# Forget gates of an attention layer: the 16 weight columns made the stationary operand, the result turned afterwards

## The chip, the cores and the metric

The kernel runs as one program on one core of a Trainium2 chip. The metric is the device time of one execution in microseconds (us); several executions of each kernel are compared by their median.

## What is computed

The program is two blocks of a transformer in float32, for one sequence of 512 tokens with 1024 features. The first block has a dilated window attention beside a retention, an attention over a memory, and a mixture of 32 experts. The second block has two layers: the even one with a differential and a sparse attention, the odd one with the forgetting attention below; each is followed by a layer norm, an MLP of width 4096 and another layer norm. The change lies in the odd layer's forget gates:

```python
h = x @ w_in_odd[li]                       # 512 x 3088: q, k, v of 16 heads of 64, and 16 forget logits
qf, kf, vf, fl = _split(h, ODD_SPLITS)
...
log_f = jax.nn.log_sigmoid(f_logit + f_bias)
c = jnp.cumsum(log_f, axis=1).transpose(0, 2, 1)
s = jnp.einsum('bqhd,bshd->bhqs', qb, kf) + cq[..., None] - c[:, :, None, :]
p = jax.nn.softmax(jnp.where(mask, s, -jnp.inf), axis=-1)
```

## The kernel before

The kernel is written engine by engine: one function per engine and stage, which issue instructions in a fixed order, and semaphores that are counted in a first pass over the program. `T` is TensorE, `A` ScalarE, `V` VectorE, `G` GpSimd, `Y` SyncE, which issues the loads.

**Projections.** A product in float32 is made of three products in the type fp32r: features and weights are each split into a high part and a low part (what the high part leaves), and high x high, low x high and high x low are summed in the same bank (`three`, `products`, L448 to L455). `FH` and `FL` are the features' parts, features on the partitions, in 8 blocks of 128 features with 512 tokens each. Weights come in units of 4 blocks x 512 columns: SyncE loads unit u into one of four buffers `R`, ScalarE copies it to the high part (`act_cut`, L434), VectorE subtracts for the low part (`dve_cut`, L442), in one of two split buffers `W`. SyncE, ScalarE and VectorE wait in `sp_send` and the two cuts for buffers to come free. Two units make one panel of 512 output columns. `projecting` takes the four tiles of 128 tokens through the first unit, then through the second: 4 x 12 matmuls each, with a tile's features stationary (128 columns) and the weights moved (512 columns). Each tile fills one of eight PSUM banks.

**Banks.** `Banks.take` hands out banks in rotation. Each set of banks named by `of` has its own turn: projections take from banks 0 to 5 (PANELS), transposes of finished panels from 6 and 7 (FLIPS), and everything else from all eight (ALL). A bank may be taken again when its last user's reader is done, and TensorE waits for that at the take. In the traces' tile names the banks are `PB`.

**The odd layer's projection** (`pe_odd`, `act_odd`, `dve_odd`) has six panels p: q in 0 and 1, k in 2 and 3, v in 4 and 5. ScalarE copies tiles of panels 0 to 3 out of PSUM (L3041), TensorE turns them during the next panel (`pe_turn`, L467), ScalarE stores them (L645); VectorE copies panels 4 and 5 (L3076).

**The forget gates** come after panel 0. The 16 weight columns `k.o_wf`, 8 blocks of 128x16 in plain float32, are not part of the panels. TensorE takes one bank from ALL and, for each tile of 128 tokens, makes 16 products (8 blocks, high and low features read as plain float32) with the tile's features stationary and the 16 columns moved (`group`, L460). The logits lie in the bank with tokens on partitions. `dve_forget` (L3104 to L3120) adds the bias and, with two steps of ScalarE (L3050, L3052), forms the log of the sigmoid in a widened table `o_lw`. After panel 1, TensorE sums it over the tokens with a triangular table, 4 plain float32 products of 512 columns into a bank of ALL, and `dve_forget_sums` (L3127, L3128) reads that bank. On VectorE these two lines stand behind both weight splits of panel 2. GpSimd then makes a selection table (L3135). The attention takes banks from ALL for scores, transposed weights and sums. The output projection `out_odd` starts inside it; VectorE adds its tiles to `X` (L1284) and does the layer norm; TensorE turns the result into the features of the last MLP, banks 6 and 7, and ScalarE and VectorE split them (L542, L552). The MLP's first products take banks from ALL.

```python
        if p == 0:
            bank = k.banks.take(T, ("flog",), k.dve_step.at("forget", "logits"))
            T.wait_ge(*k.c6_in.at(3))
            for i in range(NT):
                at = slice(128 * i, 128 * i + 128)
                ins = group(te, bank[:, 16 * i:16 * i + 16],
                            [(F[:, c, at].bitcast(F32), k.o_wf[:, c, :]) for F in (k.FH, k.FL) for c in range(KT)])
```

Of the kernel before, what the change touches and what calls it, by code (L numbers as in the profile page):

```python
# [284 lines left out]
class Kernel:  # L285


    def __init__(self, nc, ctx, a, out):
# [12 lines left out]
        def both(name, shape):  # L301
# [16 lines left out]
        self.mem_feats = [nc.alloc_sbuf_tensor_at(name, [P, KT, 256], FR, offset=self.z_at + 4 * at)  # L318
                          for name, at in (("mem_hi", 4096), ("mem_lo", 6144))]
        self.pickr = nc.alloc_sbuf_tensor_at("pickr", [P, 16, P], FR, offset=self.z_at + 4 * 13056)  # L320
        self.om = [sb(f"om{i}", [P, D]) for i in range(2)]
        self.ident = sb("ident", [P, P])
        self.mh = sb("mh", [P, 32])
# [153 lines left out]


def projecting(k, name, p, u0, nt, ready, until, between=None, after=None, by_tile=False, steps=None, early=0,
               feats=None):  # L480

# [6 lines left out]
    for n, (half, i) in enumerate(steps):  # L490
# [12 lines left out]
        if half == 1:  # L503
            ins.then_inc(*done.tick(name, p, i))
            if after:
                after(i)
        elif not [x for x in steps[n + 1:] if x[0] == 0]:
            ins.then_inc(*k.w.half_used.tick(u))
            if between:
                between()  # L510
        if n < early:
            yield
            if n == early - 1:
                for tile in {i for _, i in steps[:early]}:
                    k.banks.release((name, p, tile))
# [2431 lines left out]
def odd_views(k):  # L2947
# [3 lines left out]
    k.o_vf = Z[:, 8192:12288].rearrange("p (i d) -> p i d", i=4)  # L2951
    k.o_wf = Z[:, 12288:12416].rearrange("p (k n) -> p k n", k=8)
    k.o_lf, k.o_fb = Z[:, 12416:12480], Z[:, 12480:12496]
    k.o_lw = Z[:, 15616:16128].rearrange("p (i m) -> p i m", i=4)
    k.o_tri = Z[:, 13056:13952]
    k.o_pick = Z[:, 13056:15104].rearrange("p (h m) -> p h m", h=16)
# [21 lines left out]
def pe_odd(k):  # L2978
    T, te, u0 = k.T, k.T.e, k.start["odd"]

    def turn(p):
        return lambda i: pe_turn(k, ("odd", p, i), k.nsp[i], k.panel_a.at("odd", p, i))

    for p in range(6):
        pe_project(k, "odd", p, u0 + 2 * p, NT, lambda i: featured(k, ("ln", 1), i),
                   lambda i: (k.panel_a if p < 4 else k.panel_v).at("odd", p, i), after=(turn(p - 1) if 1 <= p < 5 else None))
        if p == 0:
            bank = k.banks.take(T, ("flog",), k.dve_step.at("forget", "logits"))
            T.wait_ge(*k.c6_in.at(3))
            for i in range(NT):  # L2990
                at = slice(128 * i, 128 * i + 128)
                ins = group(te, bank[:, 16 * i:16 * i + 16],
                            [(F[:, c, at].bitcast(F32), k.o_wf[:, c, :]) for F in (k.FH, k.FL) for c in range(KT)])
            ins.then_inc(*k.pe_step.tick("forget"))
        if p == 1:
            bank = k.banks.take(T, ("fsum",), k.dve_step.at("sums"))
            T.wait_ge(*k.dve_step.at("forget", "wide"))
            group(te, bank[:], [(k.o_lw[:, c, :], k.o_tri[:, 384 - 128 * c:896 - 128 * c])
                                for c in range(4)]).then_inc(*k.pe_step.tick("sums"))
# [32 lines left out]
def act_odd(k):  # L3032
    A, ae, u0 = k.A, k.A.e, k.start["odd"]
    for p in range(6):
        act_cut(k, u0 + 2 * p + 2)
        for i in range(NT):
            if p < 4:
                A.wait_ge(*k.projected.at("odd", p, i))
# [30 lines left out]
def dve_odd(k):  # L3069
    V, ve, u0 = k.V, k.V.e, k.start["odd"]  # L3070
    for p in range(6):
        dve_cut(k, u0 + 2 * p + 2)
        if p >= 4:
            for i in range(NT):
# [28 lines left out]
def dve_forget(k):  # L3103

    V, ve, tb, lf = k.V, k.V.e, k.tmp[0], k.o_lf
    l3 = lf.rearrange("p (i h) -> p i h", i=4)
    V.wait_ge(*k.c6_in.at(3))
    V.wait_ge(*k.pe_step.at("forget"))
    ve.tensor_tensor(l3, k.banks["flog",][:, 0:64].rearrange("p (i h) -> p i h", i=4),
                     k.o_fb.unsqueeze(1).to_broadcast([P, 4, 16]), ALU.add).then_inc(*k.dve_step.tick("forget", "logits"))  # L3110
    V.wait_ge(*k.dve_step.at("forget", "logits"))
    V.settle(ve.tensor_scalar(tb[:, 0:64], lf, -1.0, None, ALU.mult))
# [198 lines left out]
```

## Time and profile before

| what | value |
|---|---|
| runs | 2473.95, 2473.32, 2466.71 us; median 2473.32 |
| profiled execution | 2466.64 us, of it span from first to last instruction 2465.3 us |
| TensorE matmul busy | 2285.8 us, 93% of the span |
| TensorE weight loads, busy | 1686.8 us, 68% |
| VectorE, ScalarE, GpSimd busy | 1044.6, 703.7 and 95.4 us |
| mean granted TensorE clock | 0.960 of full |

PE is TensorE (PEld its weight loads), DVE VectorE, ACT ScalarE, POOL GpSimd, SP SyncE. Times in the trace are microseconds from the start of the span, durations of single instructions may overlap on TensorE, since matmuls are pipelined and their ends are modelled. Names of a matmul are written result <- moved, stationary; its shape is stationary (rows * columns), then moved. The granted clock is a share of full speed: its two levels are 1.2 and 2.4 GHz.

### The profile page before, as it was taken

To read this page: it belongs to the slowest core of one execution; us is meant where nothing else is said; L and a number is where in the kernel's file an instruction comes from. 1 tells how busy PE (TensorE), PEld (TensorE's weight loads), DVE (VectorE), ACT (ScalarE), POOL (GpSimd) and SP (SyncE) were. 2 spreads that over 40 slices of the span, in tenths; PEclk is the share of its full clock that TensorE was granted. 3 is DMA by queue.
4 is the path that set the end of the run, shared out by engine and by line. 5 is a ranking of instruction groups with operands and counts; after the bars stand their busy time and mean duration, and the time that the engine had idled before them with its cause. 6 is when DMAs were issued, how large, how long until landed. Compare 5 with 4: busy or idle time off the path is not lost.

```text
span 2465.3 us, 28479 instructions
## 1 busy us (share of the span) xinstructions
PE 2285.8 (93%) x11871; PEld 1686.8 (68%) x11871; DVE 1044.6 (42%) x1904; ACT 703.7 (29%) x1188; POOL 95.4 (4%) x96
## 2 busy tenths in 40 slices
PE   8998899979989889899788899999899998999998
PEld 7866687754434333587555688888787776888886
DVE  5347365342323222534576633344511455442334
ACT  4333354311100000223355223132113362331330
POOL 2001001010000000000000000000000000000000
PEclk9989999989999999999888999999989999999999
DMA  5232243259999999522100333322222201323220
GB/s 193 86 135 73 95 154 120 80 220 411 426 428 426 427 428 428 181 70 69 69 1 2 103 104 102 103 86 102 81 70 85 86 2 35 109 97 103 91 97 34
DMA packets 106740, 370.34 MB, mean 150 GB/s; under 512 B 15040, under 2 KB 20672, under 8 KB 94320
## 3 DMA queue, kind: packets, MB, share of 16 engines
q1 hardware_dynamic: 103584, 361.65, 39.0%
q0 software_dynamic: 3024, 6.83, 0.9%
q8 instruction: 96, 1.57, 0.3%
q14 instruction: 36, 0.29, 0.0%
HBM read 368.38 MB, written 4.19 MB: 151 GB/s over the span
## 4 chain that ended last, share of the span: by engine, by line
PE 80%; DMA 9%; DVE 7%; ACT 2%; issue 1%; POOL 0%; SPq 0%; DVEq 0%; ACTq 0%; POOLq 0%
PE PB L450 53%; PE PB L1892 9%; PE PB L467 5%; PE PB L460 4%; PE PB L766 4%; PE PB L658 3%; DMA FL_raw<-in_w_exp_gate 3%; DMA FH_raw<-in_w_exp_gate 3%; DMA Z<-in_w_exp_gate 1%; DMA W_raw<-in_w_exp_down 1%; PE PB L782 1%; DVE W L442 1%; PE PB L663 1%; ACT W L434 1%; ACT nsp L692 1%
## 5 line engine op out<-in xcount | busy, mean ns | idle before, releaser
L442 DVE TENSOR_TENSOR W<-R,W 128x2048 fp32r<-128x2048 f32 (+1 forms) x128 | 291.3, 2277 | 668.2 <-ACT W L434 668.1
L450 PE MATMUL PB<-W,FH 128*128 128x512 f32 (+1 forms) x1792 | 557.4, 393 | 16.7 <-DVE FL L820 6.7
L434 ACT ACTIVATE W<-R 128x2048 fp32r<-128x2048 f32 (+1 forms) x128 | 243.4, 1902 | 670.6 <-PE PB L450 666.5
L450 PEld LDWEIGHTS PB<-W,FH 128*128 128x128 f32 x1792 | 331.6, 190 | 86.4 <-DVE FL L820 8.0
L450 PE MATMUL PB<-W,hid 128*128 128x512 f32 x1536 | 350.3, 389 | 5.1 <-DVE W L442 3.3
L450 PE MATMUL PB<-W,FL 128*128 128x512 f32 (+1 forms) x896 | 348.0, 388 | 0.0
L450 PEld LDWEIGHTS PB<-W,hid 128*128 128x128 f32 x1536 | 287.9, 188 | 66.4 <-DVE W L442 4.2
L450 PE MATMUL PB<-FH,W 128*128 128x512 f32 (+1 forms) x1152 | 326.2, 369 | 1.5 <-DVE FL L552 1.5
L450 PEld LDWEIGHTS PB<-FH,W 128*128 128x128 f32 x1152 | 211.3, 192 | 36.6 <-DVE FL L552 1.8
L450 PE MATMUL PB<-FL,W 128*128 128x512 f32 (+1 forms) x576 | 212.2, 368 | 0.0
L450 PEld LDWEIGHTS PB<-W,FL 128*128 128x128 f32 x896 | 169.5, 189 | 34.9
L1892 PE MATMUL PB<-R,om 128*64 128x512 f32 x320 | 150.4, 626 | 16.4 <-DMA FL_raw<-in_w_exp_gate 9.2
L1892 PE MATMUL PB<-Z,om 128*64 128x512 f32 x304 | 124.4, 610 | 0.8 <-issue 0.8
L450 PEld LDWEIGHTS PB<-FL,W 128*128 128x128 f32 x576 | 110.6, 192 | 17.5
L692 ACT ACTIVATE nsp<-nsp,stat 128x512 f32<-128x512 f32 (+3 forms) x146 | 83.4, 572 | 102.5 <-DVE stat L674 102.4
L467 PEld LDWEIGHTS PB<-ident,nsp 128*128 128x128 f32 x674 | 81.6, 150 | 42.5 <-issue 28.4
L467 PE MATMUL PB<-ident,nsp 128*128 128x128 f32 x674 | 104.4, 284 | 5.1 <-ACT nsp L692 2.8
L658 PE MATMUL PB<-Z 64*128 64x512 f32 (+4 forms) x416 | 97.8, 534 | 10.7 <-DVE Z L807 5.1
L766 PE MATMUL PB<-ptr,Z 128*64 128x128 f32 (+1 forms) x768 | 82.5, 290 | 22.6 <-ACT ptr L716 12.1
L674 DVE CUSTOM_DVE_ANT_0 nsp<-PB,Z 128x512 f32<-128x512 f32 (+3 forms) x146 | 69.1, 511 | 62.1 <-PE PB L658 46.2
L1965 ACT ACTIVATE tmp_r<-PB 128x512 fp32r<-128x512 f32 x32 | 17.4, 594 | 262.7 <-PE PB L1892 262.7
L766 PEld LDWEIGHTS PB<-ptr,Z 128*64 128x64 f32 (+1 forms) x768 | 62.0, 149 | 41.7 <-issue 29.7
(329 smaller groups left out, 2632.9 us busy)
## 6 DMA issues: line engine op xcount, KB each, us to landing
R<-in_mlp_w_up SPq DMA_DIRECT2D x32, 1024.0 KB, 5.3
R<-in_mlp_w_down SPq DMA_DIRECT2D x32, 1024.0 KB, 5.0
Z<-in_w_exp_down SPq DMA_DIRECT2D x14, 2048.0 KB, 29.3
Z<-in_w_exp_up SPq DMA_DIRECT2D x13, 2048.0 KB, 35.2
R<-in_w_exp_gate SPq DMA_DIRECT2D x11, 2048.0 KB, 33.8
W_raw<-in_w_exp_up SPq DMA_DIRECT2D x10, 2048.0 KB, 31.5
R<-in_w_exp_up SPq DMA_DIRECT2D x9, 2048.0 KB, 30.9
R<-in_w_in SPq DMA_DIRECT2D x12, 1024.0 KB, 5.8
```

The source lines that it names most:

```text
L434: k.A.e.activation(w.splits[w.split_of[u]][0][:, 0:m], w.rows(u), ACT.Copy).then_inc(*w.hi.tick(u))
L442: k.V.e.tensor_tensor(wl[:, 0:m], w.rows(u), wh[:, 0:m].bitcast(F32), ALU.subtract).then_inc(*w.lo.tick(u))
L450: ins = te.matmul(bank, l, r, start=(start and n == 0), stop=(stop and n == len(terms) - 1), skip_group_check=True)
L460: ins = te.matmul(bank, l, r, start=(n == 0), stop=(n == len(pairs) - 1))
L467: ins = k.T.e.transpose(bank[0:s.shape[1], 128 * n:128 * n + m], s, k.ident[0:m, 0:m])
L658: ins = k.T.e.matmul(bank[:, 0:t.n], t.q, t.keys, start=True, stop=(t.more is None))
L663: k.T.e.matmul(bank[:, 0:t.n], *t.more, start=False, stop=True).then_inc(*k.scored.tick(*t.key))
L674: V.e.tensor_tensor_reduce(ns[:, 0:t.n], k.banks[("scores",) + t.key][:, 0:t.n], t.tab, 1.0, FAR, ALU.add, ALU.min, peak(k, m)).then_inc(* ...
L692: k.A.e.activation(ns[:, 0:t.n], ns[:, 0:t.n], ACT.Exp, bias=peak(k, m), scale=-1.0, accum_out=t.den).then_inc(*k.exped.tick(*t.key))
L766: ins = T.e.matmul(k.banks["sums", *t.bank[0]][t.rows, at], l, r, start=first, stop=last, skip_group_check=True)
L782: ins = T.e.matmul(bank[rows, 128 * c:128 * c + 128], col, k.ident[:], start=True, stop=True, skip_group_check=True)
L1892: ins = T.e.matmul(bank[64 * side:64 * side + 64, :], lhs[:, 128 * c + 64 * side:128 * c + 64 * side + 64], ws[side][:, c, at], start=(c = ...
```

## The change

The 16 columns of weights are split like the panels' weights, by ScalarE (high part) and VectorE (low part), into two small buffers `forget_w` at a free place of `Z`. After panel 0, TensorE makes 8 x 3 = 24 fp32r products with 16 weight columns stationary and all 512 tokens of a block moved, into 16 partitions of one bank taken from ALL. VectorE copies the 16x512 to `o_gates`. After the first two tiles of panel 1 (`behind`, with n = 1), TensorE takes a second bank of ALL and transposes four pieces of 16x128, so that the logits again have tokens on partitions, 128 columns apart. `dve_forget` reads them from there.

```diff
+        self.forget_w = [nc.alloc_sbuf_tensor_at(name, [P, KT, 16], FR, offset=self.z_at + 4 * at)
+                         for name, at in (("forget_hi", 16128), ("forget_lo", 16256))]
...
 def projecting(k, name, p, u0, nt, ready, until, between=None, after=None, by_tile=False, steps=None, early=0,
-               feats=None):
+               feats=None, behind={}):
...
+        if n in behind:
+            behind[n]()
         if n < early:
...
+    k.o_gates = k.tmp[0][0:16, 512:1024]
...
+    def turn_gates():
+        bank = k.banks.take(T, ("flog",), k.dve_step.at("forget", "logits"))
+        T.wait_ge(*k.dve_step.at("forget", "copied"))
+        flips(k, bank, [k.o_gates[:, 128 * i:128 * i + 128] for i in range(NT)]).then_inc(*k.pe_step.tick("forget"))
+
     for p in range(6):
         pe_project(k, "odd", p, u0 + 2 * p, NT, lambda i: featured(k, ("ln", 1), i),
-                   lambda i: (k.panel_a if p < 4 else k.panel_v).at("odd", p, i), after=(turn(p - 1) if 1 <= p < 5 else None))
+                   lambda i: (k.panel_a if p < 4 else k.panel_v).at("odd", p, i), after=(turn(p - 1) if 1 <= p < 5 else None),
+                   behind=({1: turn_gates} if p == 1 else {}))
         if p == 0:
-            bank = k.banks.take(T, ("flog",), k.dve_step.at("forget", "logits"))
-            T.wait_ge(*k.c6_in.at(3))
-            for i in range(NT):
-                at = slice(128 * i, 128 * i + 128)
-                ins = group(te, bank[:, 16 * i:16 * i + 16],
-                            [(F[:, c, at].bitcast(F32), k.o_wf[:, c, :]) for F in (k.FH, k.FL) for c in range(KT)])
-            ins.then_inc(*k.pe_step.tick("forget"))
+            bank = k.banks.take(T, ("gates",), k.dve_step.at("forget", "copied"))
+            T.wait_ge(*k.dve_step.at("forget", "parts"))
+            terms, (wh, wl) = [], k.forget_w
+            for c in range(KT):
+                terms += three((wh[:, c, :], wl[:, c, :]), (k.FH[:, c, :], k.FL[:, c, :]))
+            products(te, bank[0:16, :], terms, True, True).then_inc(*k.pe_step.tick("gates by head"))
...
+        if p == 0:
+            A.wait_ge(*k.c6_in.at(3))
+            ae.activation(k.forget_w[0][:], k.o_wf, ACT.Copy).then_inc(*k.act_step.tick("forget", "high"))
...
+        if p == 0:
+            V.wait_ge(*k.act_step.at("forget", "high"))
+            ve.tensor_tensor(k.forget_w[1][:], k.o_wf, k.forget_w[0][:].bitcast(F32), ALU.subtract).then_inc(
+                *k.dve_step.tick("forget", "parts"))
         dve_cut(k, u0 + 2 * p + 2)
...
+    V.wait_ge(*k.pe_step.at("gates by head"))
+    ve.tensor_copy(k.o_gates, k.banks["gates",][0:16, :]).then_inc(*k.dve_step.tick("forget", "copied"))
     V.wait_ge(*k.c6_in.at(3))
     V.wait_ge(*k.pe_step.at("forget"))
-    ve.tensor_tensor(l3, k.banks["flog",][:, 0:64].rearrange("p (i h) -> p i h", i=4),
+    ve.tensor_tensor(l3, k.banks["flog",][:].rearrange("p (i m) -> p i m", i=4)[:, :, 0:16],
```

Where the instructions now stand is shown at three places of TensorE's order; rows of the change have line numbers two to five higher. `PB2` is bank 2, `W0` and `W1` are the split buffers, `FH` and `FL` the features' parts, `Z` holds tables and weights.

Behind panel 0, before (the last of panel 0, the gates' products, the first of panel 1):

```order
L450 MATMUL PB5<-W0_51,FL_50 128x512
L460 MATMUL PB2<-Z,FH_49 128x16 [waits c6_in,panel_a]
L460 MATMUL PB2<-Z,FH_49 128x16 x7
L460 MATMUL PB2<-Z,FL_50 128x16 x8
L450 MATMUL PB0<-W1_52,FH_49 128x512 [waits added,w_lo]
```

and with the change, to the transposes within panel 1 (three of the 24 products, then the starts of panel 1's tiles):

```order
L452 MATMUL PB5<-W0_51,FL_50 128x512
L452 MATMUL PB2<-FH_49,forget_hi_59 16x512 [waits dve_step,panel_a]
L452 MATMUL PB2<-FL_50,forget_hi_59 16x512
L452 MATMUL PB2<-FH_49,forget_lo_60 16x512
L452 MATMUL PB0<-W1_52,FH_49 128x512 [waits added,w_lo]
L452 MATMUL PB1<-W1_52,FH_49 128x512 [waits added]
L469 MATMUL PB3<-ident,tmp0 128x16 [waits dve_step,panel_a]
L469 MATMUL PB3<-ident,tmp0 128x16 x3
L452 MATMUL PB2<-W1_52,FH_49 128x512 x2
```

The row with 7 or 8 of the same stands for 128 products in all before; there are 24 now, and four transposes into PB3 further down.

Between panel 1 and panel 2, before (the last transposes, the sums over tokens, panel 2's first products):

```order
L467 MATMUL PB7<-ident,nsp3 128x128 [waits panel_a,piece]
L467 MATMUL PB7<-ident,nsp3 128x128 x3
L460 MATMUL PB3<-Z 128x512 [waits dve_step,panel_a]
L460 MATMUL PB3<-Z 128x512 x3
L450 MATMUL PB4<-W1_52,FH_49 128x512 [waits w_lo]
```

and with the change:

```order
L469 MATMUL PB7<-ident,nsp3 128x128 [waits panel_a,piece]
L469 MATMUL PB7<-ident,nsp3 128x128 x3
L462 MATMUL PB4<-Z 128x512 [waits dve_step]
L462 MATMUL PB4<-Z 128x512 x3
L452 MATMUL PB4<-W1_52,FH_49 128x512 [waits dve_step,w_lo]
```

The sums moved from PB3 to PB4, and panel 2's first tile, which is PB4 in both, has a wait for VectorE more.

At the last MLP, before (the last transposes of the features, in PB6 and PB7, and the first products):

```order
L467 MATMUL PB6<-ident,X 128x128 [waits feat_lo,ln_out]
L467 MATMUL PB6<-ident,X 128x128 x3
L467 MATMUL PB7<-ident,X 128x128 [waits feat_lo]
L467 MATMUL PB7<-ident,X 128x128 x3
L450 MATMUL PB2<-FH_49,W1_52 128x256 [waits res,w_lo]
```

and with the change:

```order
L469 MATMUL PB6<-ident,X 128x128 [waits feat_lo,ln_out]
L469 MATMUL PB6<-ident,X 128x128 x3
L469 MATMUL PB7<-ident,X 128x128 [waits feat_lo]
L469 MATMUL PB7<-ident,X 128x128 x3
L452 MATMUL PB7<-FH_49,W1_52 128x256 [waits res,w_lo,feat_lo]
```

The MLP's first bank moved from PB2 to PB7, the bank of the transposes just ahead, with a wait for the features' low parts.

## Rows read from the trace of the kernel before

**Rows 1.** The page: busy time of the engines, and the chain by engine.
```profile
PE 2285.8 (93%) x11871; PEld 1686.8 (68%) x11871; DVE 1044.6 (42%) x1904; ACT 703.7 (29%) x1188; POOL 95.4 (4%) x96
PE 80%; DMA 9%; DVE 7%; ACT 2%; issue 1%; POOL 0%; SPq 0%; DVEq 0%; ACTq 0%; POOLq 0%
```

**Rows 2.** Source line L460, 1780 to 1870: duration ns min/median/max, first and last start, shapes.
```profile
L460 PE MATMUL PB<-Z,FH x64: 177/374/374, 1806.2 to 1826.4; 128*128 128x16 f32 x64
L460 PE MATMUL PB<-Z,FL x64: 262/374/374, 1807.9 to 1829.8; 128*128 128x16 f32 x64
L460 PE MATMUL PB<-Z x8: 592/592/697, 1856.3 to 1859.4; 128*128 128x512 f32 x8
```

**Rows 3.** Chain of waits, 1780 to 1960: start us, us, what.
```profile
1806.31 23.87 PE PB L460 x128
1830.19 15.39 PE PB L450 x60
...
1860.04 13.64 PE PB L450 x60
```

**Rows 4.** Windows: PE, PEld (DVE, ACT, POOL) busy, clock, DMA; the first, L1892 alone.
```profile
600.00:650.00 50.00, 40.97 (x190) 13.27 (x186) 1.00 1.01 426
...
1805.90:1830.20 24.30, 24.30 (x131) 24.23 (x130) 2.29 (x1) 2.40 (x2) 0.00 (x0) 0.58 0.14 44
1830.20:1850.00 19.80, 19.80 (x85) 16.22 (x86) 4.14 (x9) 5.50 (x8) 0.00 (x0) 0.91 0.08 20
```

**Rows 5.** Timeline of TensorE: start us, us, what, count [idle before <-releaser].
```profile
1805.47 0.62 PE L450 MATMUL PB<-W,FH 128*128 128x512 f32 x2
...
1806.15 1.85 PE L460 MATMUL PB<-Z,FH 128*128 128x16 f32 x16
...
1830.03 1.20 PE L450 MATMUL PB<-W,FH 128*128 128x512 f32 x2
...
1856.34 3.70 PE L460 MATMUL PB<-Z 128*128 128x512 f32 x8 [0.75 <-ACT nsp L3041]
1859.47 1.03 PE L450 MATMUL PB<-W,FH 128*128 128x512 f32 x2
```

**Rows 6.** Timeline of VectorE, 1780 to 1870.
```profile
1797.48 2.29 DVE L442 TENSOR_TENSOR W<-R,W 128x2048 fp32r<-128x2048 f32 x1 [9.49 <-ACT W L434]
1808.78 2.29 DVE L442 TENSOR_TENSOR W<-R,W 128x2048 fp32r<-128x2048 f32 x1 [9.01 <-ACT W L434]
1830.29 0.23 DVE L3109 TENSOR_TENSOR Z<-PB,Z 128x64 f32<-128x64 f32 x1 [19.22 <-PE PB L460]
...
1858.61 2.29 DVE L442 TENSOR_TENSOR W<-R,W 128x2048 fp32r<-128x2048 f32 x1 [11.41 <-ACT W L434]
1860.82 0.68 DVE L3127 CAST sums<-PB 128x512 fp32r<-128x512 f32 x1
1861.53 0.68 DVE L3128 TENSOR_TENSOR sums<-PB,sums 16x512 fp32r<-16x512 f32 x1
```

**Rows 7.** Timelines of VectorE and TensorE at the first output product.
```profile
2038.97 0.29 DVE L674 CUSTOM_DVE_ANT_0 nsp<-PB,Z 128x128 f32<-128x128 f32 x1
...
2040.27 0.69 PE L450 MATMUL PB<-W,FH 128*128 128x512 f32 x2 [1.45 <-ACT ptr L716]
```

**Rows 8.** Timelines of TensorE and VectorE in the output projection's second half.
```profile
2074.63 0.74 PE L450 MATMUL PB<-W,FH 128*128 128x512 f32 x2 [1.52 <-DVE X L1284]
...
2080.40 0.69 DVE L1284 SCALAR_TENSOR_TENSOR X<-X,PB 128x512 f32<-128x512 f32 x1 [0.33 <-PE PB L450]
...
2085.85 0.69 DVE L1284 SCALAR_TENSOR_TENSOR X<-X,PB 128x512 f32<-128x512 f32 x1 [0.61 <-PE PB L450]
...
2092.19 0.69 DVE L1284 SCALAR_TENSOR_TENSOR X<-X,PB 128x512 f32<-128x512 f32 x1 [0.30 <-PE PB L450]
```

**Rows 9.** Timelines of TensorE and VectorE at the last MLP's start.
```profile
2103.68 0.56 PE L450 MATMUL PB<-FH,W 128*128 128x256 f32 x1
...
2104.69 0.69 DVE L552 TENSOR_TENSOR FL<-PB,FH 128x512 fp32r<-128x512 f32 x1 [0.16 <-ACT FH L542]
```

## The prediction

> **What bounds the kernel now.** I read the page first: TensorE is busy for 93% of the span and holds 80% of the chain that ended last [rows 1]. So time taken out of TensorE's row of instructions is time off the end, unless a wait replaces it. Next I read the source line of the gates' products: 128 matmuls that move 16 columns each, median 0.374 us [rows 2]. The chain of waits shows them standing on the path alone: 23.87 us between panel 0 and panel 1 [rows 3]. The windows show what they do to TensorE's clock: granted 0.58 over that block and 0.91 over the 20 us behind it; a stretch with 64-column weights that moves 512 columns holds 1.00 [rows 4]. The timelines [rows 5 to 9] then give starts for each step below. For one product of the three-term kind I take the pitch of the panels: three of them start every 0.68 us (1805.47 to 1806.15), so 0.227 us each [rows 5].
>
> **1. The block.** Removed: from 1806.15 to 1830.03, 23.88 us [rows 5]. Added in its place: 8 feature blocks x 3 terms = 24 matmuls that move 512 columns over 16-column weights, 24 x 0.227 = 5.44 us. No row shows such a matmul. Its lower end: nothing shortens the 512 columns that stream by, and the 0.227 us already hides a 128-column weight load, so I put 24 x 0.21 = 5.1 us, an estimate from that row. Its upper end is as if it ran like the plain f32 rows: two instructions per product, 0.427 us each at full clock (8 of them in 3.70 us, less the tail), so 24 x 0.85 = 20.5 us [rows 2, 5]. I take 5.44, since type and moved shape are the panels' own. Term: -18.4 us.
> The Trainium skill (TensorE: Matmul & The Clock Gate, Back-to-back issue gap) puts a warm matmul at its columns over 2.4 GHz plus 2.5 ns, which is 0.216 us here; the panels' row says 0.227. By the page the block would take 5.18 us and the sum would be 0.3 us lower.
>
> **2. The slow clock behind it.** Panel 1's first 60 matmuls take 15.39 us; 60 of panel 2's take 13.64 [rows 3]. The difference, 1.75 us, goes with the low clock if the new block streams without a gap. Term: -1.75.
>
> **3. Turning the result.** After two tiles of panel 1, four transposes are added. The nearest is four transposes of 128x128, whose issue adds 0.44 us to the row of panels; I take 0.44, between 0.1 and 0.8. They wait for nothing. VectorE's copy of 16x512 costs what its 16x512 row costs, 0.68 [rows 6], and starts when the products end: by then the split of 1808.78 is done (1811.07). So it is ready near 1812.5 of the old count, and TensorE asks for it after 24 more products, at 1817.0. The logits' bank PB3 is next wanted 12 products later, 2.7 us after the transposes; VectorE's logits take 0.23 us [rows 6]. Also hidden: ScalarE's high part and VectorE's low part of 128x128 weights, some 0.3 us each (the 128x128 row of [rows 7] is 0.29). They stand ahead of VectorE's split that ended at 1799.77 [rows 6] and is now wanted at 1811.6; if that cover were gone they would cost 0.6. Term: +0.44.
>
> **4. The banks.** One more bank is taken from the rotation of eight, so every later taker of that rotation moves by one. This costs what no line of the diff says. The sums' bank was PB3 and is now PB4. Two things follow. The sums no longer wait for ScalarE's copy out of PB3 (0.75 us idle [rows 5]). But PB4 is panel 2's first bank, so panel 2 now waits for VectorE to have read the sums, behind a weight split that VectorE must do first: 1858.61, then 1860.82, then 1861.53 + 0.68 = 1862.21 [rows 6]. None of these three hangs on the sums' matmuls, which would end 0.7 us earlier. With 0.15 us from VectorE's end to TensorE's start, panel 2 starts at 1862.36 where it started at 1859.47; since a start after a pause is a real start and the old one was queued behind slow f32 passes (first pair 1.03 us long against some 0.73), the loss is 2.6 us. Term: +2.6.
>
> **5. The same shift further on.** In the attention the waits keep their kinds, with bank numbers one higher. At the output projection three things differ. (a) Its first bank waited 1.45 us for ScalarE's copy of turned weights, until 2040.27; PB2 is now freed by VectorE's peak, which ends at 2039.26, so TensorE can start at 2039.4: -0.85 [rows 7]. (b) Tile 1 of the second half waited 1.52 us for a bank that VectorE's last addition frees. Now tile 2 meets that bank, when it is long free. VectorE, which sets the end here, gains only its own small waits for TensorE (0.33, 0.61, 0.30 us at three tiles): -1.2 [rows 8]. (c) The last MLP's first bank was PB2 and is now PB7, which holds the transposed features of the last tile. TensorE therefore waits until VectorE has read them, 2104.69 + 0.69 + 0.14 = 2105.52, where it started at 2103.68: +1.85 [rows 9].
>
> **Sum.** -18.4 - 1.75 + 0.44 + 2.6 - 0.85 - 1.2 + 1.85 = -17.3 us. Against the profiled execution's 2466.64 that is 2449.3. The three runs shown have a median of 2473.32, 6.7 above it; I carry the difference over: 2456.0.
>
> **Rivals.**
> *The clock falls all the same* (14%). 16 of 128 columns hold weights, fewer than any row shows, and there is the new pause of term 4. For it: the old block, continuously issued, lost the clock. Against it: that block moved 16 columns at a time, while 64-column weights with 512 moved keep 1.00 [rows 4]. Price: at half clock (1.2 instead of 2.4 GHz) the block takes at most twice its 5.44 us, and term 2 is not earned: -17.3 + 5.4 + 1.75 = -10.1, or 2463.2. If only the pause before panel 2 costs it the clock, one recovery: 2457.8.
> The Trainium skill (Perfetto Trace Analysis, Matmul Optimizations) says that the engine's power follows its utilization; read as the share of the array in use it would give this rival, read as back-to-back issue my forecast.
> *The bank waits don't bite* (8%): VectorE reaches the sums earlier, or TensorE's queue covers the pause. Without terms 4 and 5c the gain is some 21 us, 2451.6, or a little above. Against it: the split before the sums follows ScalarE's, which follows TensorE's last product.
> *The narrow products run like plain f32* (4%), since no row shows this type with fewer than 128 weight columns. At full clock: 20.5 - 5.44 = 15.1 us back, -2.2, about 2471: no change. At half clock: twice 20.5, 41 us, term 2 not earned, -17.3 + 35.6 + 1.75 = +20, or 2493: **slower**. The change turns slower once one product costs over 5.44/24 + 17.3/24 = 0.95 us.
> *Something behind gives back some of it* (4%): weights, sent four units ahead, or VectorE's layer norm, already the chain at the output projection, take some 7 us: 2463.
> My forecast keeps 70%.
>
> **How the numbers follow.** The likeliest is 2456.0. Its own spread is about 2.5 us from the estimates, and the runs shown lie 7 us apart by themselves, which carries the low end to 2447. The clock rival carries the high end to 2463.2. A measurement of this kernel can tell about 0.3%, 7.4 us, from no change. Forecast, missing waits, clock and most of the giving back are all beyond that: faster 0.94. The f32 case at full clock and a larger giving back make 0.03 same, the f32 case at half clock and what I have not seen 0.03 slower.
>
> **What would show it.** In the new profile: 24 matmuls of 128*16 128x512 that start 0.227 us apart at clock 1.00, about 5.4 us from panel 0 to panel 1; panel 1's first 60 matmuls in 13.6; four small transposes without idle time ahead; no TensorE wait for ScalarE before the sums, but one of 2.5 to 3 us for VectorE's line of the sums before panel 2; no wait of 1.5 us for VectorE's addition in the output projection; a wait of 1.8 us for the features' low parts before the last MLP. The forecast is wrong if the narrow products start over 0.3 us apart, if the clock falls in them, or if TensorE has a new wait outside these places.

## The result, and the profile after

| | before | after |
|---|---|---|
| median | 2473.32 us (2466.71 to 2475.32, 5 runs) | 2456.44 us (2454.54 to 2458.8, 5 runs) |
| ratio of the two | | 0.9935, 95% interval 0.9919 to 0.995 |
| profiled execution | 2466.64 us, span 2465.3 | 2456.44 us, span 2454.8 |

The change is faster by 16.9 us in the medians, 0.65%, and the interval of the ratio stays clear of 1; the 0.3% that a measurement can tell is 7.4 us. Five more runs of the same kernel (e9) gave a ratio of 0.9923 (0.9909 to 0.9937).

The page after, busy time and chain by engine, for [rows 1]:

```profile
PE 2272.5 (93%) x11771; PEld 1669.4 (68%) x11771; DVE 1045.1 (43%) x1906; ACT 703.7 (29%) x1189; POOL 95.2 (4%) x96
...
PE 78%; DMA 10%; DVE 8%; ACT 2%; issue 1%; POOL 0%; SPq 0%; DVEq 0%; ACTq 0%; POOLq 0%
```

TensorE issues 100 matmuls fewer (128 out, 24 and 4 in) and is busy for 13.3 us less. It stays the bound, with 78% of the chain where it had 80%.

The source line of the products after, for [rows 2]. The narrow weights have shape 128*16, and PEld rows are weight loads:

```profile
L452 PE MATMUL PB<-W,FH x57: 389/389/499, 1809.8 to 1835.9; 128*128 128x512 f32 x57
L452 PEld LDWEIGHTS PB<-W,FH x56: 186/188/192, 1810.0 to 1835.7; 128*128 128x128 f32 x56
...
L452 PEld LDWEIGHTS PB<-FH,forget_hi x8: 94/94/98, 1811.4 to 1816.2; 128*16 128x16 f32 x8
L452 PE MATMUL PB<-FH,forget_hi x8: 391/394/397, 1811.6 to 1816.5; 128*16 128x512 f32 x8
```

TensorE's timeline at the five places of the prediction: the block, panel 1 with the transposes, the sums and panel 2, the first output product, the last MLP, for [rows 5, 7, 9]:

```profile
1811.60 0.40 PE L452 MATMUL PB<-FH,forget_hi 128*16 128x512 f32 x1
...
1817.17 0.62 PE L452 MATMUL PB<-W,FH 128*128 128x512 f32 x2
...
1822.72 0.42 PE L469 MATMUL PB<-ident,tmp 16*128 16x16 f32 x4
1823.07 0.73 PE L452 MATMUL PB<-W,FH 128*128 128x512 f32 x2
...
1841.39 3.60 PE L462 MATMUL PB<-Z 128*128 128x512 f32 x8
1848.32 0.70 PE L452 MATMUL PB<-W,FH 128*128 128x512 f32 x2 [3.33 <-DVE sums L3148]
...
2029.54 0.70 PE L452 MATMUL PB<-W,FH 128*128 128x512 f32 x2 [0.59 <-DVE stat L679]
...
2093.10 0.58 PE L452 MATMUL PB<-FH,W 128*128 128x256 f32 x1 [1.41 <-DVE FL L557]
```

The windows over the block, over panel 1 behind it, over panel 2's start and the rest of its first 60 matmuls, and over the MLP's start, for [rows 4] (columns as there):

```profile
1811.60:1817.20 5.60, 5.60 (x26) 2.41 (x25) 2.29 (x1) 2.40 (x2) 0.00 (x0) 1.00 0.00 0
1817.20:1831.40 14.20, 14.20 (x66) 11.46 (x65) 3.07 (x10) 3.71 (x4) 0.00 (x0) 1.00 0.23 75
1848.30:1853.30 5.00, 4.98 (x15) 3.96 (x16) 0.00 (x0) 0.00 (x0) 2.72 (x2) 0.66 0.55 200
1853.30:1863.80 10.50, 10.50 (x49) 8.63 (x48) 0.67 (x1) 1.92 (x1) 0.00 (x0) 1.00 0.00 0
2093.10:2098.10 5.00, 5.00 (x23) 5.00 (x24) 2.29 (x1) 1.02 (x1) 0.00 (x0) 0.50 0.11 19
```

The chain of waits at panel 2, for [rows 3]. The path leaves TensorE at the last transposes of panel 1 and comes back by way of both splits and both lines of the sums:

```profile
1841.65 0.60 ACT nsp L3055
1842.24 0.49 ACT Z L650
1842.73 1.80 ACT W L436
1844.54 0.02 issue
1844.56 2.29 DVE W L444
1846.85 0.61 DVE sums L3147
1847.46 0.02 issue
1847.49 0.69 DVE sums L3148
1848.18 0.14 issue
1848.32 15.49 PE PB L452 x60
```

**How the executions are compared.** Ahead of the changed code every kernel is the same, yet panel 0 starts anywhere from 1782.88 to 1792.63 us in the twelve profiled executions of this study (1788.22 and 1791.30 for the same kernel). So the ends of two executions don't tell a microsecond. The stages behind panel 0 do: the same kernel profiled twice gave 643.20 and 643.18 us from the end of panel 0 to the end of the span. The table gives each stage as the difference of two starts on TensorE's timeline. "Attention" is its first score product, "output" the output projection's first product, and "MLP" the last MLP's first product.

| kernel | block | panel 1 to sums | sums to panel 2 | panel 2 to attention | attention to output | output to MLP | MLP to end | total |
|---|---|---|---|---|---|---|---|---|
| before | 23.88 | 26.31 | 3.13 | 94.20 | 86.60 | 63.41 | 361.62 | 659.15 |
| after | 5.57 | 24.22 | 6.93 | 95.48 | 85.74 | 63.56 | 361.70 | 643.20 |
| e1 shift alone | 23.75 | 25.56 | 6.93 | 96.47 | 85.74 | 63.59 | 361.60 | 663.64 |
| e2 change, no shift | 5.57 | 25.13 | 3.13 | 94.19 | 86.62 | 64.96 | 362.08 | 641.68 |
| e3 change, free banks | 5.57 | 24.22 | 3.03 | 94.19 | 85.08 | 61.96 | 360.44 | 634.49 |
| e4 swap alone | 13.84 | 25.24 | 3.13 | 94.20 | 86.60 | 63.44 | 361.92 | 648.37 |
| e5 split alone | 16.86 | 26.51 | 3.14 | 94.19 | 86.60 | 63.45 | 361.72 | 652.47 |
| e6 block twice | 11.13 | 25.12 | 3.14 | 94.19 | 86.61 | 63.46 | 361.80 | 645.45 |
| e7 sums first | 5.57 | 24.22 | 5.19 | 93.86 | 85.73 | 63.62 | 361.66 | 639.85 |
| e8 MLP's bank | 5.56 | 24.22 | 6.94 | 95.46 | 85.74 | 61.86 | 360.86 | 640.64 |
| e9 change again | 5.57 | 24.24 | 6.93 | 95.48 | 85.74 | 63.59 | 361.63 | 643.18 |
| e10 e3 again | 5.57 | 24.21 | 3.04 | 94.18 | 85.11 | 61.99 | 360.40 | 634.50 |

By stages the change gains 659.15 - 643.20 = 15.95 us.

### The profile page after: what moved, and what is told of

Read it like the earlier page. It is cut to its first block, busy times and chain, and to the rows that moved or that the text cites. A ratio compares the mean times of both kernels' runs of the same rounds, so it can differ in the third digit from the quotient of the medians.

```text
span 2454.8 us, 28285 instructions
## 1 busy us (share of the span) xinstructions
PE 2272.5 (93%) x11771; PEld 1669.4 (68%) x11771; DVE 1045.1 (43%) x1906; ACT 703.7 (29%) x1189; POOL 95.2 (4%) x96
## 4 chain that ended last, share of the span: by engine, by line
PE 78%; DMA 10%; DVE 8%; ACT 2%; issue 1%; POOL 0%; SPq 0%; DVEq 0%; ACTq 0%; POOLq 0%
PE PB L452 53%; PE PB L1897 8%; PE PB L469 5%; PE PB L771 4%; PE PB L462 3%; PE PB L663 3%; DMA Z<-in_w_exp_gate 3%; DVE W L444 1%; DMA FH_raw<-in_w_exp_gate 1%; DMA FL_raw<-in_w_exp_gate 1%; DMA Z<-in_w_exp_down 1%; DMA W_raw<-in_w_exp_down 1%; PE PB L787 1%; DMA FL_raw<-in_w_exp_down 1%; PE PB L668 1%
## 5 line engine op out<-in xcount | busy, mean ns | idle before, releaser
L452 PE MATMUL PB<-W,FH 128*128 128x512 f32 (+1 forms) x1792 | 556.9, 393 | 18.0 <-DVE FL L825 6.7
L452 PEld LDWEIGHTS PB<-W,FH 128*128 128x128 f32 x1792 | 331.9, 190 | 88.2 <-issue 8.7
L452 PE MATMUL PB<-W,hid 128*128 128x512 f32 x1536 | 350.0, 389 | 4.3 <-DVE W L444 3.3
L452 PE MATMUL PB<-W,FL 128*128 128x512 f32 (+1 forms) x896 | 348.5, 389 | 0.0
L452 PEld LDWEIGHTS PB<-W,hid 128*128 128x128 f32 x1536 | 288.0, 188 | 65.2 <-DVE W L444 4.2
L452 PE MATMUL PB<-FH,W 128*128 128x512 f32 (+1 forms) x1152 | 327.4, 370 | 2.9 <-DVE FL L557 2.9
L452 PEld LDWEIGHTS PB<-FH,W 128*128 128x128 f32 x1152 | 212.3, 193 | 38.4 <-DVE FL L557 3.6
L452 PE MATMUL PB<-FL,W 128*128 128x512 f32 (+1 forms) x576 | 212.8, 369 | 0.0
L452 PEld LDWEIGHTS PB<-W,FL 128*128 128x128 f32 x896 | 169.2, 189 | 35.1
L452 PEld LDWEIGHTS PB<-FL,W 128*128 128x128 f32 x576 | 111.2, 193 | 17.5
L679 DVE CUSTOM_DVE_ANT_0 nsp<-PB,Z 128x512 f32<-128x512 f32 (+3 forms) x146 | 69.1, 510 | 64.3 <-PE PB L663 48.1
```

The source lines that it names most:

```text
L452: ins = te.matmul(bank, l, r, start=(start and n == 0), stop=(stop and n == len(terms) - 1), skip_group_check=True)
L679: V.e.tensor_tensor_reduce(ns[:, 0:t.n], k.banks[("scores",) + t.key][:, 0:t.n], t.tab, 1.0, FAR, ALU.add, ALU.min, peak(k, m)).then_inc(* ...
```

## The experiments

The theory is the prediction's: the narrow products run at the panels' pace and keep the clock, and the bank that is taken once more costs waits at three places. The rivals are the prediction's own, and one on why the old block was slow.

### e1: the shift of the banks alone

The kernel before, with the turn of the eight banks moved on by one ahead of the sums, and nothing else of the change.

```diff
+            k.banks.turn[Banks.ALL] += 1
             bank = k.banks.take(T, ("fsum",), ...)
```

> The kernel before, with the rotation of eight banks moved by one ahead of the sums over tokens, and nothing else. Theory A (the shift has a price of its own): TensorE waits 3.3 us for VectorE's reading of the sums ahead of panel 2, the clock falls behind that pause and costs 1.85 us in panel 2's first 60 matmuls, the first output product waits 0.6 instead of 1.45, the second half of the output projection loses its 1.5 us wait, the last MLP waits 1.4 to 1.8 us: from panel 1's start to the end some 2 to 4 us more than before, so about 2475.5 to 2477 beside 2473. Theory B (gained and lost waits cancel): within 1 us of before.

Measured: median 2476.21 us (10 runs) against 2472.68 (17 runs), ratio 1.001, interval 1.0 to 1.0019; by stages 4.49 us longer than before. The waits are those of the change. TensorE's waits in e1, from 1780 us on (us in total, times, longest):

```profile
PE PB L450 <- DVE sums L3129: 3.3, 1, 3.3
PE PB L450 <- DVE FL L552: 1.4, 1, 1.4
```

and its windows over panel 2's start and behind it:

```profile
1872.30:1877.30 5.00, 5.00 (x12) 3.94 (x13) 0.00 (x0) 0.00 (x0) 2.70 (x2) 0.50 0.55 202
1877.30:1888.30 11.00, 11.00 (x49) 9.06 (x48) 0.20 (x1) 1.92 (x1) 0.00 (x0) 0.98 0.00 0
```

So a bank's number alone, with no arithmetic changed, costs 4.49 us by stages, a little over the 2 to 4 expected, and 3.5 us in the medians. 2.27 of them are panel 2 behind the pause (94.20 to 96.47), with the lower clock at its start; no term of the prediction's sum had that, only its clock rival.

### e2, e3: the change without the shift, and with a free bank

e2 takes the block's bank and the transposes' bank from the rotation of banks 6 and 7, and moves the turn so that the sums have PB3 again and every later bank is that of before. e3 moves it by six instead of one: the sums get PB0.

```diff
-            bank = k.banks.take(T, ("gates",), k.dve_step.at("forget", "copied"))
+            bank = k.banks.take(T, ("gates",), k.dve_step.at("forget", "copied"), of=Banks.FLIPS)
...
+            k.banks.turn[Banks.ALL] += 1
             bank = k.banks.take(T, ("fsum",), ...)
```

> The change with the gates' product and the transposes in banks 6 and 7, and the rotation of eight set so that the sums lie in PB3 and every later bank is the one it was before. Theory A: the gain is that of the block, its clock and the transposes alone, 18.3 + 1.75 - 0.35 = 19.7 us, so 2453.5 beside 2473, with the old waits back (0.75 us before the sums, 1.45 and 1.52 us in the output projection) and no wait ahead of panel 2 or the last MLP. Theory B: no better than the change, 2456 to 2457.

> As the kernel with no shift, but with the rotation set so that the sums lie in PB0, long free and not wanted in panel 2 before its third tile, and the last MLP begins in PB0. Theory A: no wait before the sums (0.75 less), none ahead of panel 2, none for the features, and a shorter first wait in the output projection: 1 to 3 us below the kernel with no shift, 2451 to 2452.5 beside 2473. Theory B: the same as the change, 2456.

e2: median 2457.81 us (6 runs), ratio 0.9929 (0.9912 to 0.9946); by stages 17.47 us less than before, 1.5 less than the change. Theory A's 19.7 us were missed by the stages, and the median lies nearer to Theory B's 2456 to 2457 than to 2453.5: the medians don't tell e2 from the change. Panel 2 is back at 94.19. One stage is odd: from the output projection's first product to the MLP, where e2 has the banks and waits of before, 64.96 us instead of 63.41. There the clock fell, in this execution, after a pause of 1.45 us that before has too (clock 1.00 there):

```profile
2028.90:2040.10 11.20, 11.20 (x47) 8.54 (x48) 1.29 (x4) 1.08 (x3) 0.00 (x0) 0.85 0.01 1
```

With before's 63.41 there e2 would gain 19.0 us. Two of its six runs (2448.85 and 2451.61 us, mean clock 0.965 and 0.964) are well below the other four (0.959 to 0.961); whether they lacked this fall isn't known, since one execution was profiled.

e3: median 2449.61 us (5 runs), ratio 0.9905 (0.989 to 0.992); by stages 24.66 us less than before, 8.7 less than the change. What TensorE still waits for in e3, from 1780 us on:

```profile
PE PB L469 <- DVE FL L557: 14.3, 4, 6.5
PE PB L452 <- DVE W L444: 3.3, 2, 1.7
PE PB L663 <- DVE Z L3095: 0.9, 1, 0.9
PE PB L771 <- ACT ptr L721: 0.3, 1, 0.3
```

The waits for the sums, for the turned weights, for VectorE's `X` and for the features' low parts are all gone. Against e2, which differs by the offset alone, e3 is 7.19 us shorter by stages, where 1 to 3 were expected: 1.01 up to panel 2's start, 1.54 at the first output product, 3.00 up to the MLP and 1.64 behind it. Some 1.55 of the 3.00 are e2's own fall of the clock. So the bank numbers are worth about half as much as the change itself.

### e4, e5, e6: what made the old block slow

The change does two things at once to the products: it splits the weights, and it swaps which operand is stationary. e4 is e2 with the swap alone (16 plain float32 products, 16 columns stationary, 512 moved).

```diff
-            terms, (wh, wl) = [], k.forget_w
-            for c in range(KT):
-                terms += three((wh[:, c, :], wl[:, c, :]), (k.FH[:, c, :], k.FL[:, c, :]))
-            products(te, bank[0:16, :], terms, True, True).then_inc(...)
+            group(te, bank[0:16, :], [(k.o_wf[:, c, :], F[:, c, :].bitcast(F32)) for F in (k.FH, k.FL)
+                                      for c in range(KT)]).then_inc(...)
```

> As the kernel with no shift, but the 16 weight columns stay plain float32 and are the stationary operand of 16 products (8 blocks, high and low features) that move 512 columns; the split weights are made and not read. Theory A (type sets the pitch: two instructions of two passes per plain float32 product, as in the sums): 16 x 0.85 = 13.7 us for the block, clock 1.00, so 8 us more than the kernel with no shift. Rival C (narrow weights of any type stream at the pitch of 0.23): 16 x 0.23 = 3.7 us, faster than with split weights. Rival D (few columns of the array in use lose the clock): up to 27 us.

Block 13.84 us, as Theory A has it; a single run, 2464.5 us. Line L462 in e4:

```profile
L462 PEld LDWEIGHTS PB<-FH,Z x16: 93/97/97, 1814.4 to 1820.5; 128*16 128x16 f32 x16
L462 PE MATMUL PB<-FH,Z x16: 592/592/603, 1814.4 to 1820.9; 128*16 128x512 f32 x16
```

and its windows over the block and the 14 us behind it:

```profile
1814.40:1828.20 13.80, 13.80 (x33) 3.02 (x32) 2.29 (x1) 2.40 (x2) 0.00 (x0) 1.00 0.24 76
1828.20:1842.40 14.20, 14.20 (x65) 11.47 (x65) 2.86 (x10) 3.71 (x4) 0.00 (x0) 1.00 0.00 1
```

Two instructions for each product, 13.84 / 32 = 0.43 us each, and the clock stays at 1.00.

e5 is the kernel before with the split alone: features stationary, 16 columns moved, 96 products.

```diff
+            wh, wl = k.forget_w
...
-                at = slice(128 * i, 128 * i + 128)
-                ins = group(te, bank[:, 16 * i:16 * i + 16],
-                            [(F[:, c, at].bitcast(F32), k.o_wf[:, c, :]) for F in (k.FH, k.FL) for c in range(KT)])
+                terms, at = [], slice(128 * i, 128 * i + 128)
+                for c in range(KT):
+                    terms += three((k.FH[:, c, at], k.FL[:, c, at]), (wh[:, c, :], wl[:, c, :]))
+                ins = products(te, bank[:, 16 * i:16 * i + 16], terms, True, True)
```

> The kernel before, with the 16 weight columns split into high and low parts as in the change, but the features stay stationary and the 16 columns are moved: 96 fp32r products of 128*128 stationary and 16 moved instead of 128 plain float32 matmuls' worth. No transposes, banks as before. This is the split without the swap. Theory A (the block is paced by loading 128 stationary columns per product, and its 16 moved columns at a time lose the clock): at full clock one costs about 0.11 us, at half clock 0.21; the clock falls some microseconds into the block, so the block takes 16 to 20 us instead of 23.88, and panel 1's first 60 matmuls are slowed as before (about 15.4 us instead of 13.64). Rival C (the slow part was only the float32 type): 96 products at under 0.11 us each with the clock at 1.00, block 10 us or less, panel 1 at full speed.

Block 16.86 us, as Theory A has it; a single run, 2465.77 us. Line L452 in e5:

```profile
L452 PEld LDWEIGHTS PB<-forget_hi,FH x32: 188/333/333, 1811.7 to 1828.1; 128*128 128x128 f32 x32
L452 PE MATMUL PB<-forget_hi,FH x32: 172/361/361, 1811.9 to 1828.2; 128*128 128x16 f32 x32
```

and its windows over the block in two parts and over panel 1's start:

```profile
1811.90:1818.00 6.10, 6.10 (x47) 6.06 (x45) 2.29 (x1) 2.40 (x2) 0.00 (x0) 0.81 0.02 2
1818.00:1828.80 10.80, 10.80 (x53) 10.80 (x52) 0.00 (x0) 0.00 (x0) 0.00 (x0) 0.50 0.31 97
1828.80:1844.20 15.40, 15.40 (x61) 12.57 (x62) 2.19 (x9) 3.71 (x4) 0.00 (x0) 0.87 0.00 0
```

The weight loads are busy for the whole of the second window: with 128 columns loaded for each 16 moved, the load sets the pace. At the higher clock these products start 0.112 us apart (32 starts from 1812.07 to 1815.54), at the lower, from 1815.78 on, 0.213 us. At the higher clock throughout the 96 would take 10.7 us; losing it costs 6 us in the block and panel 1's slow start besides (26.51 us to the sums).
The Trainium skill (TensorE: Matmul & The Clock Gate, LDWEIGHTS) gives a weight load its columns over 1.2 GHz, 0.107 us for 128, close to the 0.112 of pitch here.

e6 is e2 with the 24 narrow products made twice, the second time afresh into the same bank.

```diff
             products(te, bank[0:16, :], terms, True, True)
+            products(te, bank[0:16, :], terms, True, True)
```

> The kernel of e2 (the change, with the gates' bank taken from the flips' rotation and the sums back in PB3) with the 24 narrow products made twice, the second time starting afresh in the same bank: 48 products with 16 stationary columns and 512 moved. Theory A (the narrow products cost 0.232 us each and hold the full clock for as long as they stream): block 11.1 us, granted clock 1.00 in the block and behind it, panel 1 to the sums unchanged at about 25.1 us, end 5.6 us later than e2's by stages. Rival B (a narrow block only escapes the fall of the clock because it is short): clock under 0.9 in the second half of the block or in panel 1, block over 12 us or panel 1 at least 1 us longer.

Block 11.13 us, which is 48 x 0.232; a single run, 2459.27 us. Its windows over the block and behind it:

```profile
1812.20:1823.30 11.10, 11.10 (x50) 4.64 (x49) 2.29 (x1) 2.40 (x2) 0.00 (x0) 1.00 0.29 94
1823.30:1837.50 14.20, 14.20 (x66) 11.46 (x65) 3.06 (x10) 3.71 (x4) 0.00 (x0) 1.00 0.00 1
```

Panel 1 behind it is as long as in e2 (25.12 and 25.13 us), so Rival B is refuted. The narrow block doesn't escape the lower clock by being short; it holds the higher one for 11 us. That the old block lost it goes with which operand was moved and not with the type: e5 loses it with the new type, e4 keeps it with the old. The swap changes two things together, the columns moved at a time (16 to 512) and the columns loaded for them (128 to 16), and no run separates these.

### e7, e8: the two new waits taken away one by one

e7 is the change with VectorE's two lines of the sums ahead of the second weight split of panel 2.

```diff
+        if p == 1:
+            dve_forget_sums(k)
         dve_cut(k, u0 + 2 * p + 3)
...
-        elif p == 1:
-            dve_forget_sums(k)
```

> The change, with VectorE's two lines of the sums put ahead of the second weight split of panel 2 instead of behind it. The PE pause before panel 2 shortens from 3.33 us to about 1.5 (the sums' matmuls end, two VectorE operations of 0.68 us, 0.15 us to start). Theory A (the length of the pause is the wait for the split, and the clock falls for the pause): from the sums' first matmul to panel 2's first 5.1 us instead of 6.93, and panel 2's first 60 matmuls in 13.64 us at clock 1.00 instead of 15.49: about 3.6 us less than the change. Rival B (any pause after the float32 sums costs the clock): 1.8 us less from the pause alone, first 60 still about 15.4 us. Rival C (the split comes late now and TensorE waits for it in panel 2's second unit): a new wait of 1 us or more on VectorE's W in panel 2, gain under 1 us.

Median 2454.98 us (4 runs), ratio 0.9924 (0.9907 to 0.994); by stages 3.35 us less than the change, 1.74 of it in the pause and 1.62 behind it. TensorE at the sums in e7:

```profile
1840.44 3.60 PE L462 MATMUL PB<-Z 128*128 128x512 f32 x8
1845.63 0.70 PE L452 MATMUL PB<-W,FH 128*128 128x512 f32 x2 [1.59 <-DVE sums L3148]
```

its chain at panel 2, and the window behind the pause:

```profile
1845.63 13.87 PE PB L452 x60
...
1845.60:1850.60 5.00, 4.97 (x22) 4.16 (x23) 2.21 (x1) 0.00 (x0) 4.71 (x3) 1.00 0.31 74
```

The pause is 1.59 us instead of 3.33, and after it the clock stays at 1.00. The split that now comes second is not missed: no new wait stands in panel 2 (Rival C). The medians (2454.98 against 2454.34 and 2456.44 for the change) don't show 3.35 us; only the stages do.

e8 is the change with the turn moved on by one at the start of the last MLP, so that its first bank is PB0.

```diff
+    if layer == 1:
+        k.banks.turn[Banks.ALL] += 1
     for c in range(2):
```

> The change, with the rotation of all eight banks moved on by one at the start of the last MLP, so that its first products take PB0 and not PB7, the bank of the last tile's transposed features. Everything ahead as in the change. Theory A (TensorE's 1.41 us wait for the features' low parts is what term 5c cost, and the clock falls for it): no wait there; from VectorE's last tile of the output projection to the MLP's first product about 11.5 us instead of 13.24; end 1.7 to 2.8 us earlier than the change by stages after the output projection's start. Rival B (the wait is hidden anyway, since the second unit or its other banks wait for the same reader): the start comes earlier, but a wait of the same size stands within the first 24 products or the first bank reuse behind, and the stage from the MLP's first product to the end grows by as much.

A single run, 2453.84 us; by stages 2.56 us less than the change. TensorE's last transposes and first MLP product in e8:

```profile
2089.75 1.94 PE L469 MATMUL PB<-ident,X 128*128 128x128 f32 x8 [0.65 <-DVE FL L557]
2091.34 0.56 PE L452 MATMUL PB<-FH,W 128*128 128x256 f32 x1
```

The wait of 1.41 us is gone, the stage ahead is 1.70 us shorter and the one behind it 0.84 us: in the first 5 us of the MLP e8 has a clock of 0.62 and issues 30 matmuls, where the change has 0.50 and 23. The wait didn't bring the clock down, as Theory A had it: the clock is at 0.50 in the 5 us ahead of the MLP's first product in before, the change and e8 alike. In the change it comes back later.

```profile
2091.30:2096.30 5.00, 5.00 (x30) 5.00 (x28) 3.53 (x3) 2.57 (x3) 0.00 (x0) 0.62 0.01 3
```

### e9, e10: the change and e3 once more, side by side

> The change itself once more, beside e10 on the same chip. Theory A (its 3.3 us pause before panel 2 costs the clock each time): sums' first matmul to panel 2's first 6.9 us, panel 2's first 60 matmuls about 15.5 us, panel 0's end to the end of the span 643 us within 1. Rival B (the fall of the clock there was an accident of one execution): the first 60 in 13.64. Median 2456 within 3 us.

> The kernel of e3 once more, beside e9 on the same chip. Theory A (a kernel with the narrow products and none of the bank waits gains some 8.7 us over the change by stages): panel 0's end to the end of the span 634.5 us within 1, median 6 to 9 us under e9's. Rival B (much of e3's lead was the scatter of executions): median within 3 us of e9's.

Both kernels unaltered, on one chip: e9 2454.34 us (2449.06 to 2459.57, 5 runs), e10 2446.98 us (2444.72 to 2451.13, 4 runs), 7.4 us apart in the medians, before 2473.26 (9 runs). Ratios to before: 0.9923 (0.9909 to 0.9937) and 0.9893 (0.9878 to 0.9909). Each stage of either repeats its first profile within 0.07 us, the clock of 0.66 behind the 3.33 us pause too:

```profile
1851.50:1856.50 5.00, 5.00 (x15) 3.97 (x16) 0.00 (x0) 0.00 (x0) 2.66 (x2) 0.66 0.55 201
```

e3's kernel beats before and the change, by stages both times by 8.7 us over the change.

## Why the prediction was right

The predicted 2456.0 us stands against 2456.44. Part of that closeness is luck. The sum was 17.3 us and the stages give 15.95, which from the median before would be 2457.4; that the median after is 1 us lower is within the scatter of its runs (2454.54 to 2458.8). Carrying over the 6.7 us between the profiled execution and the median was right: that execution was early before it came to the changed code, with panel 0 at 1782.88 us where all others have 1787 or more. By its terms:

| term | predicted | measured | from |
|---|---|---|---|
| 1. block | -18.4 | -18.31 | before, after |
| 2, 3. slow clock behind it, transposes | -1.31 | -1.18 | before, e2 |
| 4. sums' bank | +2.6 | +4.18 | e2, after |
| 5a. first output product | -0.85 | -0.86 | before, after |
| 5b. output projection | -1.2 | -1.55 | before, e8 |
| 5c. MLP's first bank | +1.85 | +1.78 | e8, after, before |
| sum | -17.3 | -15.95, by rounding | |

**Terms 1 to 3** hold. The pitch was 5.57 / 24 = 0.232 us where 0.227 was taken, and the clock never fell in the block or behind it. The four transposes add 0.58 us where 0.44 was taken: from the last product ahead of them (1822.40) to the first behind (1823.07) it is 0.67 us instead of 0.23, and the next 12 products take 2.86 us, where the same 12 take 2.72 in before. That leaves 1.18 + 0.58 = 1.76 us for the slow clock, and 1.75 was taken. The Trainium skill's figure (TensorE: Matmul & The Clock Gate, Back-to-back issue gap), 0.216 us, is not met by any row shown here; 0.232 is further from it than the panels' 0.227.

**Term 4 is the step that was mis-sized.** Its mechanism was right: panel 2 started 0.14 us behind VectorE's line of the sums, in the order split, L3147, L3148. Its start was right too, 2.89 us later than in e2 (24.22 + 6.93 against 25.13 + 3.13), as the rows gave (1862.36 against 1859.47); the wait itself was 3.33 us, where the signs said 2.5 to 3. Wrong was the sentence that the loss is 2.6 us, because it stopped at panel 2's start. Behind the pause the granted clock is 0.66 over 5 us, and the first 60 matmuls take 15.49 us. e7, with a pause half as long, has the full clock and takes 13.87 for them (before's 13.64 are counted from 1860.04, 0.57 us behind panel 2's first start). The stage differs by as much, 95.48 - 93.86 = 1.62 us, and 2.6 + 1.6 is the 4.2 measured. The prediction had named this as the second case of its clock rival, one recovery more, at 2457.8, and gave that rival 14% in all. This case is what happened, in all four executions with the 3.33 us pause, and not the forecast's full clock; that 2456.44 is nearer to 2456.0 than to 2457.8 is luck.

**Term 5a** hit: the wait is now 0.59 us, on VectorE's peak (L679). **5b** was a little better than its three small waits. **5c** had the right wait and the right size, by a route that was half seen: the start moves by 1.70 us, the longer low clock costs 0.84 more, and a wait of 0.8 us for VectorE's `X` (L2918) that before has within the MLP disappears with the same shift (the stage MLP to end is 0.76 us shorter in e8 than before): 1.70 + 0.84 - 0.76 = 1.78. The wait is 1.41 us, where the signs said 1.8, and that the two parts that weren't foreseen nearly cancel is luck. The wait for `X`, from TensorE's waits in before:

```profile
PE PB L450 <- DVE X L2918: 0.8, 1, 0.8
```

**The rivals.** Bank waits that don't bite are refuted by e1, where they bite alone. Products that run like plain float32 are refuted by the pitch, and e4 gives the price of one: two instructions of 0.43 us, 13.84 us for 16. The 24 products would have taken 20.8 us at that, where the rival had 20.5. A clock that falls in the narrow block is refuted by e6. Nothing behind gave back some of it: from the output projection on, the change takes 0.23 us more than before (63.56 + 361.70 against 63.41 + 361.62), which is terms 5b and 5c. Read as the share of the array in use, the rule of the Trainium skill that the engine's power follows its utilization (Perfetto Trace Analysis, Matmul Optimizations) does not agree with the trace: 16 of 128 columns held 1.00 for 11 us in e6, and full 128-column weights with 16 moved fell to 0.50 in e5. Read as matmuls issued back to back it doesn't cover e5 either, since the profile has no idle time between its products. Whether another reading of it fits, no run here was made to tell.

One argument against the clock rival was weaker than the prediction had it. The 64-column products that kept the clock at 1.00 in before start in pairs, so that two of 64 columns run side by side:

```profile
606.25 0.59 PE L1892 MATMUL PB<-FL_raw,nsp 128*64 128x512 f32 x1
606.25 0.59 PE L1892 MATMUL PB<-W_raw,nsp 128*64 128x512 f32 x1
```

They said little about an array with few columns in use. The change's own block, e4 and e6 are the first rows that do.

## What to carry to other kernels

When many products share few columns, make the few columns stationary and stream the many: it saves weight loads (24 instead of 128 for the products here), and here it kept TensorE's clock where moving 16 columns at a time lost it. In a kernel with rotating banks, an edit that takes one bank more renumbers all that follow, so list who reads each bank that is now met first: here the shift alone cost 4.5 us (e1), and with the banks chosen well the kernel was 8.7 us faster than the change (e3), half of what the change itself gave. A pause of TensorE is priced with the clock behind it, and a reader of a bank that stands behind a long operation on its engine is worth moving ahead of it: 3.35 us by stages in e7.

## What the runs showed of the hardware

- **The clock held in a nearly empty array and fell in a full one.** 24 or 48 products with 16 columns stationary and 512 moved: 1.00 (after, e6). Plain float32 of the same shape: 1.00 (e4). 128 columns stationary and 16 moved: 0.58 over the block in before, and in e5 0.50 over its last 10.8 us, without idle time in the profile.
- **After a pause the clock may fall, and the same pause doesn't always do it.** 3.33 us: fell each time (after, e1, e8, e9). 1.59 us: didn't (e7). 1.45 us at the first output product: stayed at 1.00 in before, e4, e5 and e6, 0.85 over 11 us in e2, where the stage was 1.55 us longer. Why e2 differs is open.
- **A weight load of 16 columns takes 94 ns, of 128 columns 188 ns** in the profile's records at the full clock: 0.84 ns a column between the two, which would leave some 80 ns for a load of no columns (an estimate from these two). The Trainium skill's columns over 1.2 GHz (TensorE: Matmul & The Clock Gate, LDWEIGHTS) fits the slope and not the length of one record.
- **The narrow product's pitch (0.232 us) is a little longer than the full one's (0.227)** for the same 512 columns moved, although its weight load is half as long. No run here tells why.
- Not tried: e7 and e8 in one kernel. By stages they would come to 643.20 - 3.35 - 2.56 = 637.3 us, 2.8 more than e3 (an estimate that takes the two gains to add up).
